# A decoder layer with 32 experts: the expert loop's body cut from four quads to two, and the dummy products of the last quads placed anew

## The reference, cut to what matters

```
for g in range(N_GROUPS):
    hid = (silu(einsum('nd,edf->nef', hf, w_gate[g]))
           * einsum('nd,edf->nef', hf, w_up[g]) * combine[:, g, :, None])
    out = out + einsum('nef,efd->nd', hid, w_down[g])
...
return rmsnorm(x, final_norm_g)
```

## Time and profile before

| | us |
|---|---|
| median of 3 runs | 451.15 |
| lowest and highest | 450.29, 452.39 |
| the profiled execution, as timed | 450.17 |
| its span in the profile | 448.2 |
| mean granted TensorE clock in it | 0.97 of 2.4 GHz |
| TensorE busy (3286 products and as many weight loads) | 409.5 |
| VectorE busy | 189.2 |
| ScalarE busy | 156.5 |
| mean transfer rate | 312 GB/s over the span |

### The profile page before, as it was taken

How to read it: one execution, slowest core, us unless ns; L and a number is a source line. 1 busy time by engine, 2 the same in 40 slices (tenths; PEclk the granted TensorE clock), 3 DMA queues, 4 the chain that set the end, 5 groups by cost and what they waited for, 6 DMA issues and landing times.

```text
span 448.2 us, 8018 instructions
## 1 busy us (share of the span) xinstructions
PE 409.5 (91%) x3286; PEld 310.3 (69%) x3286; DVE 189.2 (42%) x352; ACT 156.5 (35%) x303; POOL 39.0 (9%) x80
## 2 busy tenths in 40 slices
PE   7999999999999999999999989989869838978974
PEld 6999999899999999999898634434333413622621
DVE  3674766776558945745555311221211202102103
ACT  5734564656439635475727210000000000001013
POOL 4010232323100000000400200000000000000000
PEclk9999999999999999999999999999998959969988
DMA  7978875666783677795499999999999999999973
GB/s 234 294 208 267 260 246 183 214 226 202 255 268 125 223 266 250 222 348 182 150 358 368 377 424 422 421 420 420 420 420 422 420 424 420 421 418 409 409 305 140
DMA packets 56233, 139.62 MB, mean 312 GB/s; under 512 B 5350, under 2 KB 39174, under 8 KB 46982
## 3 DMA queue, kind: packets, MB, share of 16 engines
q1 hardware_dynamic: 55840, 138.31, 83.0%
q10 hardware_dynamic: 358, 0.80, 0.5%
HBM read 138.06 MB, written 1.05 MB: 310 GB/s over the span
## 4 chain that ended last, share of the span: by engine, by line
PE 72%; DMA 12%; SPq 9%; ACT 2%; issue 1%; DVE 1%; POOLq 0%; POOL 0%; DVEq 0%; ACTq 0%
PE proj L1291 13%; PE proj L1292 13%; PE proj L1293 13%; PE proj L1578 7%; DMA moe_pair<-in_expert_w_up_dram 6%; SPq L387 6%; PE score L1601 5%; PE score L1533 4%; DMA moe_pair<-in_expert_w_down_dram 4%; SPq L379 2%; PE attno L1635 2%; PE proj L1559 2%; PE attno L1371 1%; PE probt L1291 1%; PE probt L1293 1%
## 5 line engine op out<-in xcount | busy, mean ns | idle before, releaser
L872 DVE TENSOR_TENSOR w_lo<-w_raw,w_hi 128x1024 fp32r<-128x1024 f32 x64 | 78.5, 1231 | 41.0 <-ACT w_hi L622 40.7
L622 ACT ACTIVATE w_hi<-w_raw 128x1024 fp32r<-128x1024 f32 x64 | 67.8, 1060 | 36.5 <-PE proj L1293 18.1
L1291 PE MATMUL proj<-hT_hi,w_hi 128*128 128x256 f32 x232 | 67.5, 291 | 1.8 <-DVE hT_lo L863 1.5
L1292 PE MATMUL proj<-hT_lo,w_hi 128*128 128x256 f32 x232 | 65.6, 283 | 0.0
L1293 PE MATMUL proj<-hT_hi,w_lo 128*128 128x256 f32 x232 | 65.6, 283 | 0.0
L1578 PE MATMUL proj<-moe_pair,moe_x 128*32 128x512 f32 x384 | 50.7, 675 | 15.9 <-DMA moe_pair<-in_expert_w_up_dram 15.9
L1211 DVE TENSOR_TENSOR moe_x<-score,gains_moe 128x256 f32<-128x256 f32 x32 | 13.6, 425 | 93.8 <-PE score L1533 93.8
L815 ACT ACTIVATE hid<-proj 128x256 f32<-128x256 f32 x8 | 3.1, 385 | 138.8 <-PE proj L1578 115.5
L1291 PEld LDWEIGHTS proj<-hT_hi,w_hi 128*128 128x128 f32 x232 | 44.4, 191 | 5.5 <-issue 3.6
L1292 PEld LDWEIGHTS proj<-hT_lo,w_hi 128*128 128x128 f32 x232 | 44.4, 192 | 0.0
L1293 PEld LDWEIGHTS proj<-hT_hi,w_lo 128*128 128x128 f32 x232 | 44.4, 191 | 0.0
(11 more groups left out here) (281 smaller groups left out, 782.0 us busy)
## 6 DMA issues: line engine op xcount, KB each, us to landing
moe_pair<-in_expert_w_down_dram SPq DMA_DIRECT2D x26, 1024.0 KB, 26.1
moe_pair<-in_expert_w_gate_dram SPq DMA_DIRECT2D x24, 1024.0 KB, 19.0
moe_pair<-in_expert_w_up_dram SPq DMA_DIRECT2D x24, 1024.0 KB, 21.0
w_raw<-in_w_in_dram SPq DMA_DIRECT2D x33, 512.0 KB, 4.5
moe_pair<-in_expert_w_gate_dram SPq DMA_DIRECT2D x16, 512.0 KB, 10.9
moe_pair<-in_expert_w_up_dram SPq DMA_DIRECT2D x16, 512.0 KB, 11.4
moe_pair<-in_expert_w_down_dram SPq DMA_DIRECT2D x12, 512.0 KB, 7.0
w_raw<-in_xattn_wkv_dram SPq DMA_DIRECT2D x8, 512.0 KB, 3.9
```

The costliest lines, as they stand in the source:

```text
L622: act.activation(w_hi[g % NS][:], w_raw[:, g % NW], ACT.Copy).then_inc(hi_done, 1)
L872: dve.tensor_tensor(w_lo[g % NS][:], w_raw[:, g % NW], w_hi[g % NS][:].bitcast(F32), ALU.subtract)\
L1291: pe.matmul(ps, a[0], b[0], start=start, stop=False, skip_group_check=True)
L1292: pe.matmul(ps, a[0], b[1], start=False, stop=False, skip_group_check=True)
```

## The change

1. The loop's body is two quads instead of four. Quad 0 stands alone ahead of the loop, the body holds quads 1 and 2 and is run three times (quads 1 2, 3 4, 5 6), and the last quad follows. `trips` now counts passes of two quads, less two; TensorE, VectorE and ScalarE add one to it, SP does not, since its loop still begins with quad 3.
2. TensorE reads `trips` in `first_quad`, behind the gate and up products, instead of behind quad 2.
3. The expressions for slots, experts and counters follow: what was a constant in quads 1 and 2 is now computed from the loop's counter.
4. The 14 dummy products ahead of quad 6 are gone. The 4 dummy products of 128 columns in the last quad are 1 of 512 columns (`warm_wide`). Behind the last quad's transposes and ahead of its down products there are 2 more of 512 columns.

```diff
-    WARM_LOOP, WARM_LAST = 14, 4
+    WARM_UP, WARM_DOWN = 1, 2
...
-    BODY_QUADS = 4
-    BODIES, BODY_CHUNKS = QUADS // BODY_QUADS, BODY_QUADS * MOE_CHUNKS
+    PAIR_CHUNKS = 2 * MOE_CHUNKS
+    ROUND_PAIRS = QUADS // 2
     SLOTS = 24
-    LAST_QUAD = BODY_QUADS - 1
+    LAST_QUAD = 1
...
-            LAST = LAST_QUAD * MOE_CHUNKS
-            for i in range(SLOTS, LAST):
+            for i in range(SLOTS, SLOTS + MOE_CHUNKS):
                 sp.wait_ge(chunk_used, user_before(i))
-                load_whole(i, 0)
+                load_whole(i, 2)
...
-            with sp.Fori(0, turns) as turn:
-                for i in range(LAST, LAST + BODY_CHUNKS):
-                    sp.wait_ge(chunk_used, turn * BODY_CHUNKS + user_before(i))
-                    load_whole(i % BODY_CHUNKS, (turn + i // BODY_CHUNKS) % BODIES)
+            with sp.Fori(0, more) as turn:
+                for i in range(SLOTS + MOE_CHUNKS, SLOTS + MOE_CHUNKS + PAIR_CHUNKS):
+                    sp.wait_ge(chunk_used, turn * PAIR_CHUNKS + user_before(i))
+                    load_whole(i, (turn * 2 + i // MOE_CHUNKS) % QUADS)
...
+            def warm_wide(bank, times):
+
+                for _ in range(times):
+                    pe.matmul(bank[:].rearrange("p (n q) -> p n q", n=4), ident[:],
+                              ident[:].unsqueeze(1).broadcast_to([P, 4, P]), start=True, stop=True)
...
                         if q == LAST_QUAD and kh and j:
-                            warm(SC[0], WARM_LAST)
+                            warm_wide(SC[0], WARM_UP)
...
                 gate_up_by_columns(0, 0, first_in, PJ[0][:, FE:2 * FE])
+                pe.wait_ge(trips_set, 1)
+                more = pe.value_load(trips[0:1, 0:1], min_val=ROUND_PAIRS - 2, max_val=ROUND_PAIRS * ROUNDS - 2)
                 transposes(0, hid_halves)
...
                 gate_up_by_columns(LAST_QUAD, n, last_in, LAST_UP)
                 transposes(n, hid_halves)
+                warm_wide(PJ[0], WARM_DOWN)
                 pe.wait_ge(hidT_sb, n + 1)
...
-            first_quad()
-            for q in range(1, LAST_QUAD):
-                whole_quad(q, q, 0)
-            pe.wait_ge(trips_set, 1)
-            turns = pe.value_load(trips[0:1, 0:1], min_val=BODIES - 1, max_val=BODIES * ROUNDS - 1)
-            with pe.Fori(0, turns) as turn:
-                whole_quad(LAST_QUAD, turn * BODY_QUADS + LAST_QUAD, turn)
-                for q in range(LAST_QUAD):
-                    if q == LAST_QUAD - 1:
-                        warm(PJ[0], WARM_LOOP)
-                    whole_quad(q, turn * BODY_QUADS + (BODY_QUADS + q), turn + 1)
-            last_quad(turns * BODY_QUADS + LAST_QUAD)
+            more = first_quad()
+            with pe.Fori(0, more + 1) as turn:
+                whole_quad(1, turn * 2 + 1, turn * 16 + 16)
+                whole_quad(0, turn * 2 + 2, turn * 16 + 16)
+            last_quad(more * 2 + 3)
```

More of the change, by code:

```diff
@@ L104, in hybrid_layer @@
     GU_CHUNKS, MOE_CHUNKS = KD, KD + KF * 2
-    BODY_QUADS = 4
-    BODIES, BODY_CHUNKS = QUADS // BODY_QUADS, BODY_QUADS * MOE_CHUNKS
+    PAIR_CHUNKS = 2 * MOE_CHUNKS
+    ROUND_PAIRS = QUADS // 2
     SLOTS = 24
-    LAST_QUAD = BODY_QUADS - 1
+    LAST_QUAD = 1
     def slot_of_chunk(i):
         return i % SLOTS
-    def landed(i, body):
-        q = i // MOE_CHUNKS
-        return body * 32 + (0, 16, 16, 32)[q]
     def user_before(i):
@@ L368, in load_half, with load_whole @@
                 sp.dma_start(w_raw[:, g % NW], halves[g]).then_inc(w_in_sem[g % NW], 16)
-            def load_whole(i, body):
-                q, c = divmod(i, MOE_CHUNKS)
-                s, e0 = slot_of_chunk(i), (body * BODY_QUADS + q) * QE
+            def load_whole(i, quad):
+                s, c, e0 = slot_of_chunk(i), i % MOE_CHUNKS, quad * QE
                 if c < GU_CHUNKS:
@@ L399, in load_first @@
                 if i >= MOE_CHUNKS:
-                    load_whole(i, 0)
+                    load_whole(i, 1)
                 elif i < GU_CHUNKS:
@@ L472, in _ @@
             load_first(23)
-            LAST = LAST_QUAD * MOE_CHUNKS
-            for i in range(SLOTS, LAST):
+            for i in range(SLOTS, SLOTS + MOE_CHUNKS):
                 sp.wait_ge(chunk_used, user_before(i))
-                load_whole(i, 0)
+                load_whole(i, 2)
             sp.wait_ge(trips_set, 1)
-            turns = sp.value_load(trips[0:1, 0:1], min_val=BODIES - 1, max_val=BODIES * ROUNDS - 1)
-            with sp.Fori(0, turns) as turn:
-                for i in range(LAST, LAST + BODY_CHUNKS):
-                    sp.wait_ge(chunk_used, turn * BODY_CHUNKS + user_before(i))
-                    load_whole(i % BODY_CHUNKS, (turn + i // BODY_CHUNKS) % BODIES)
+            more = sp.value_load(trips[0:1, 0:1], min_val=ROUND_PAIRS - 2, max_val=ROUND_PAIRS * ROUNDS - 2)
+            with sp.Fori(0, more) as turn:
+                for i in range(SLOTS + MOE_CHUNKS, SLOTS + MOE_CHUNKS + PAIR_CHUNKS):
+                    sp.wait_ge(chunk_used, turn * PAIR_CHUNKS + user_before(i))
+                    load_whole(i, (turn * 2 + i // MOE_CHUNKS) % QUADS)
             for c in range(MOE_CHUNKS):
-                sp.wait_ge(chunk_used, turns * BODY_CHUNKS + user_before(LAST + c))
+                sp.wait_ge(chunk_used, more * PAIR_CHUNKS + user_before(3 * MOE_CHUNKS + c))
                 load_last(c)
@@ L819, in expert_quad @@
                 act.activation(y0_sb[:], SC[0][:], ACT.Copy).then_inc(y_act, 1)
-            for q in range(LAST_QUAD):
-                expert_quad(q)
+            expert_quad(0)
             act.wait_ge(trips_set, 1)
[L824 to L828, removed]
+            more = act.value_load(trips[0:1, 0:1], min_val=ROUND_PAIRS - 2, max_val=ROUND_PAIRS * ROUNDS - 2)
+            with act.Fori(0, more + 1) as turn:
+                expert_quad(turn * 2 + 1)
+                expert_quad(turn * 2 + 2)
+            expert_quad(more * 2 + 3, GU_CHUNKS - 2)
             act.dma_start(fin_g[:], final_norm_g.rearrange("(a n) -> a n", a=1).broadcast_to([P, D])).then_inc(fin_in, 16)
@@ L832, in _ @@
                 for t in range(TT):
-                    act.wait_ge(back_ps[t][half], turns * BODY_QUADS + BODY_QUADS)
+                    act.wait_ge(back_ps[t][half], more * 2 + 4)
                     squares(FINAL_NORM, ACC[t][half][:], t, half, fin_rows)
@@ L1232, in expert_quad, with experts_of @@
                 dve.tensor_copy(y1_sb[:], SC[1][:]).then_inc(y_dve, 1)
[L1234 to L1239, removed]
+            def experts_of(quad):
+                return bass.ds(quad * QE, QE)
+            expert_quad(0, experts_of(0), experts_of(1))
             dve.wait_ge(trips_set, 1)
[L1241 to L1248, removed]
+            more = dve.value_load(trips[0:1, 0:1], min_val=ROUND_PAIRS - 2, max_val=ROUND_PAIRS * ROUNDS - 2)
+            with dve.Fori(0, more + 1) as turn:
+                quads = [(turn * 2 + i) % QUADS for i in range(1, 4)]
+                for i in range(2):
+                    expert_quad(turn * 2 + i + 1, experts_of(quads[i]), experts_of(quads[i + 1]))
+            expert_quad(more * 2 + 3, experts_of(QUADS - 1), up=LAST_UP)
             dve.wait_ge(fin_in, 16)
@@ L1564, in gate_up_by_columns, with gate_up_whole @@
                                     op.then_inc(chunk_used, 1)
-            def gate_up_whole(q, n, body):
+            def gate_up_whole(q, n, arrived):
                 for c in range(GU_CHUNKS):
                     i = q * MOE_CHUNKS + c
-                    pe.wait_ge(moe_in[slot_of_chunk(i)], landed(i, body))
+                    pe.wait_ge(moe_in[slot_of_chunk(i)], arrived)
                 for k in range(KD):
@@ L1663, in first_quad, with whole_quad @@
                 results(0)
-            def whole_quad(q, n, body):
-                gate_up_whole(q, n, body)
+                return more
+            def whole_quad(q, n, arrived):
+                gate_up_whole(q, n, arrived)
                 transposes(n, hid_by_rows)
```

3 lines of the change are left out of this document (1 added, 2 removed).

## The result

The changed kernel takes 448.3 us (median of 6 runs, 447.77 to 449.28), the kernel before 450.72 (6 runs, 450.15 to 452.39): a ratio of 0.9948, with a 95% interval of 0.9932 to 0.9964. A second comparison on another occasion gave 0.9958 (0.9944 to 0.9973).

A forecast was written before the change was run, and what follows sets the result against it. Weight transfers were taken to set the pace, with only the end worth gaining: loop 0 and clock 0.65 us gave 450.17 - 0.65 = 449.5 profiled, 450.5 on the runs' median scale; range 449.0 to 452.4.

The forecast's parts named there:

- the loop's new shape: Expert part's loop: entering, branching back, possibly late loads and dropped dummies are covered by waits; 0 at the kernel's end.
- the second rival: End of the weights: five instruction fetches fall away or move, so weights land 1.1 us earlier, 449.4; chance 0.12.
- The clock's term: Last quad's down products: two wide dummies keep TensorE's clock up, so the last down group starts 0.65 us earlier.
- the first rival: Last quad: nothing moves, as the clock falls anyhow or mostly had not fallen before; 451.1 us, chance 0.21.
- The 14 dummies ahead of quad 6: Ahead of quad 6: they lie in the wait for weights and bought no faster clock; removing them costs 0.
- Entering the loop, and going back: TensorE's count read in quad 0 and branches taken behind quads 2 and 4: 0, stalls covered by waits.
- The third rival: Taken branches fetch the body anew, up to six fetches of 1.1 us; two on the latest engine give 452.4; chance 0.12.
- The queue at quad 1: SP's loads at quad 1: some 8 us of transfers still queued, so the computed expressions, some 0.1 us a quad, cost nothing.
- the loop's term: The loop of two quads in the expert part: taken as 0 at the kernel's end in the forecast's sum.

The follow-up runs named there:

- e2: The changed kernel with the last quad's old dummies (four narrow ahead of the up products, none ahead of the down products): ratio 0.9951 to the kernel before.
- e6: The kernel before without the 14 dummies ahead of quad 6: ratio 0.9994 to the kernel before.
- e5: The changed kernel without the two wide dummies ahead of the down products: ratio 0.9954 to the kernel before.
- e9: The changed kernel with no dummy product in the expert part at all: ratio 0.9956 to the kernel before.
- e4: The changed kernel with 1024 tiny memsets written out on idle GpSimd, adding eight instruction fetches: ratio 1.0023 to the kernel before.
- e8: The changed kernel with 512 memsets written out on GpSimd, adding four instruction fetches: ratio 0.9964 to the kernel before.
- e7: The changed kernel with 1024 memsets on GpSimd run as 32 passes of a loop of 32: ratio 0.9942 to the kernel before.

## Why the prediction was wrong

**What failed is the step on the loop's new shape: "I take 0 at the kernel's end".** I asked of the loop what it could cost TensorE in time, found every stall covered by waits for weights, which was right, and stopped there. The step did not ask what the loop does to the thing that those waits are for. The mechanism stood in the text as the second rival, even with its count ("five fetches fall away"; 26 became 21), and with 1.1 us for the earlier landing. Measured are 1.0 us (1.4 from the entry of the expert part) in the profiles, and for the loop alone, by e2, a ratio of 0.9951: 2.2 us, with an interval of 1.6 to 2.8, where my sum had 0. So the rival, too, was priced low. Part of that is the price of one fetch: I had only the 1.1 us of the packet itself, while the packets show that it also holds up the one behind it. I gave the rival 0.12, on the ground that a fetch would have to hit "just the latest of 16". That ground was weak. Five fetches had fallen between 306 and 425 us, and the uneven end of the engines (share 0.78, then 0.49) was a sign that something delays some of them and not others; in that stretch fetches were the only traffic beside the weights.

**The clock's term, 0.65 us**: right in place, and in size as far as the runs can tell. Alone it gave 0.17% (0.77 us, interval 0.2 to 1.3). That the kernel before loses the clock every time, which the sum took for granted and the first rival doubted, is not so (e6 kept it), and in the new shape the dummies' gain is too small to measure (e5, e9).

**The 14 dummies ahead of quad 6 worth nothing**: right, within the scatter (0.9994).

**Entering the loop, and going back, cost TensorE nothing**: right. The branch as TensorE's sequencer shows it in the changed kernel, three times:

```profile
L1701 PEldq COMPARE_BRANCH  x3: 76/213/242, 308.7 to 415.0; - x3
```

0.08 to 0.24 us each, and no idle time between the gather and quad 3 (309.45 + 1.95, then 311.32). The second going back, ahead of quad 5, lies in a wait for weights, where a short stall could not be seen. The rule of the Trainium skill that a taken branch outside a window of two pages has to wait for its page ("Runtime: NRT & Kernel Launch", Instruction fetch mechanics) did not come out here: two quads are 37 KB by the prediction's count, more than two pages of 16 KB, and there was no fetch, and no stall where one could be seen. The same section gives TensorE an instruction memory of 128 KiB, larger than the other engines'; with that figure the trace agrees. What the section says against loops also came out the other way round: the body written out was the slower form.

**The third rival, slower by re-fetching**: wrong, since nothing was fetched anew. Its arithmetic, a fetch off the latest engine costs nothing and those on it cost all, is what e4 and e8 look like, at some 0.66 us a fetch there.

**The queue at quad 1**: right. SP's first load for quad 3 went out 0.4 us later, as the expert part began 0.4 us later, and the transfers' share has no gap there.

**The scale.** The profiled execution before was 0.55 us below the median of its six runs, the one after at its own median. So medians show 2.4 us where the two profiles show 1.9. The forecast stood on the median of three runs, 451.15; six gave 450.72. That is 0.4 of the 2.2 us between forecast and result; the rest has the size of the loop's term. The chance of 0.80 in the prediction was worked out for 448.9 to 453.4, not for the range that it states; the result lies below both.

## What to carry to other kernels

When transfers are the bound and every engine serves a fixed part of each of them, ask of a change not only what it does to the bytes but to the one engine that ends last; instruction fetches are such traffic, and a loop whose body is run from instructions already held takes them away. Code written out costs even on an engine that nobody waits for: 64 KB of it on an idle GpSimd cost 3.4 us here. And a stall that is covered by a wait for data is no proof that the code around it is free, as long as it has not been asked what sets the length of that wait.

## What the runs showed of the hardware that I had not expected

- Eight instruction fetches of 8 KB, 0.05% of the bytes, made the kernel 0.8% slower (1.0023 against 0.9942), while the cost of four (0.9964) is hardly clear of the scatter.
- In the full stretch a fetch also lengthened the packet of weights behind it, from 0.31 us to about 0.66 (GpSimd's) or 0.8 (TensorE's).
- With the transfer engines full, GpSimd stood still for about 0.8 us behind 128 instructions of straight code (e4), and not in a loop of 32 (e7).
- TensorE ran a body of about 37 KB three times with no further fetch between 306 and 425 us and branches of 0.08 to 0.24 us.
- The granted clock fell after waits of 2.23 and 2.24 us ahead of the down products (before, e9), and stayed up after waits of 1.29 us (e2), 1.25 us (e6) and 0.97 us (e5). What lies between was not tried.
